# Four edits to a fused three-stage float32 kernel: later out projections in the first mixer, a GpSimd addition, an order on ScalarE, a later key product

## The reference

```python
y = y.reshape(bsz, seq, D_INNER) * jax.nn.silu(z.astype(f32))
y = rmsnorm(y.reshape(bsz, seq, SSD_GROUPS, D_INNER // SSD_GROUPS), gnorm.reshape(SSD_GROUPS, -1))
return y.reshape(bsz, seq, D_INNER).astype(u.dtype) @ w_out
```

## Time and profile before

| | us |
|---|---|
| median of 3 runs (1792.98 to 1796.91) | 1793.48 |
| the profiled execution, its own time | 1795.42 |
| its span | 1793.7 |
| PE busy | 1693.6 (94%) |
| DVE busy | 1125.9 (63%) |
| ACT busy | 841.1 (47%) |
| POOL busy | 368.6 (21%) |
| mean granted clock of PE, share of full speed | 0.978 |

### The profile page before, as it was taken

How to read it: one execution, slowest core, us unless ns; L and a number is a source line. 1 busy time by engine, 2 the same in 40 slices (tenths; PEclk the granted TensorE clock), 3 DMA queues, 4 the chain that set the end, 5 groups by cost and what they waited for, 6 DMA issues and landing times.

```text
span 1793.7 us, 20988 instructions
## 1 busy us (share of the span) xinstructions
PE 1693.6 (94%) x7944; PEld 1361.2 (76%) x7944; DVE 1125.9 (63%) x1520; ACT 841.1 (47%) x1365; POOL 368.6 (21%) x299
## 2 busy tenths in 40 slices
PE   6889999999979999999988899999899999999998
PEld 5667777777757778787866678887688688888886
DVE  6668777788767475756566767777556553434343
ACT  5666565666624354435345335446354442323232
POOL 0254554455541000000006212221220200000001
PEclk9999999999989999999998999999999999999999
DMA  3634444344212222222222323222233333333332
GB/s 105 182 120 127 129 118 140 119 136 123 83 29 82 59 71 71 72 81 70 61 75 60 82 60 82 64 73 88 82 92 98 93 93 96 94 95 102 97 94 71
DMA packets 260106, 164.58 MB, mean 92 GB/s; under 512 B 26909, under 2 KB 249286, under 8 KB 258982
## 3 DMA queue, kind: packets, MB, share of 16 engines
q1 hardware_dynamic: 260006, 163.25, 31.6%
HBM read 160.86 MB, written 2.36 MB: 91 GB/s over the span
## 4 chain that ended last, share of the span: by engine, by line
PE 72%; DVE 14%; ACT 6%; issue 4%; POOL 2%; DMA 1%; SPq 0%; DVEq 0%; ACTq 0%; POOLq 0%
PE stream L79 20%; PE stream L81 20%; PE stream L80 20%; DVE weights_lo L147 2%; DVE ssd_x L987 2%; ACT weights_hi L137 1%; PE q L782 1%; PE q L1969 1%; PE q L1993 1%; PE q L79 1%; PE q L81 1%; PE q L80 1%; DVE ssd_m L1065 1%; PE q L809 1%; POOL h_sum_of_squares L220 1%
## 5 line engine op out<-in xcount | busy, mean ns | idle before, releaser
L79 PE MATMUL stream<-u_lo,weights_hi 128*128 128x512 f32 (+2 forms) x1312 | 533.7, 407 | 12.1 <-DVE u_lo L249 4.5
L81 PE MATMUL stream<-u_hi,weights_hi 128*128 128x512 f32 (+2 forms) x1312 | 516.2, 393 | 0.0
L80 PE MATMUL stream<-u_hi,weights_lo 128*128 128x512 f32 (+2 forms) x1312 | 516.0, 393 | 0.0
L147 DVE TENSOR_TENSOR weights_lo<-weights_raw,weights_hi 128x1024 fp32r<-128x1024 f32 (+4 forms) x269 | 329.4, 1226 | 274.6 <-ACT weights_hi L137 274.2
L137 ACT ACTIVATE weights_hi<-weights_raw 128x1024 fp32r<-128x1024 f32 (+4 forms) x269 | 268.8, 1001 | 462.8 <-PE stream L81 435.3
L79 PEld LDWEIGHTS stream<-u_lo,weights_hi 128*128 128x128 f32 (+2 forms) x1312 | 248.4, 189 | 78.2 <-issue 11.0
L80 PEld LDWEIGHTS stream<-u_hi,weights_lo 128*128 128x128 f32 (+2 forms) x1312 | 248.9, 190 | 54.9 <-issue 4.7
L81 PEld LDWEIGHTS stream<-u_hi,weights_hi 128*128 128x128 f32 (+2 forms) x1312 | 248.0, 189 | 55.6 <-issue 0.7
L217 POOL COPY h_sum_of_squares<-h_squares 128x512 f32<-128x512 f32 x5 | 3.3, 650 | 798.5 <-ACT h_squares L205 798.5
L79 PE MATMUL stream<-mlp_a_lo,weights_hi 128*128 128x512 f32 x256 | 100.2, 391 | 0.0
L81 PE MATMUL stream<-mlp_a_hi,weights_hi 128*128 128x512 f32 x256 | 99.7, 389 | 0.0
(11 more groups left out here) (460 smaller groups left out, 2884.5 us busy)
## 6 DMA issues: line engine op xcount, KB each, us to landing
weights_raw<-in_w_mlp_dram SPq DMA_DIRECT2D x64, 512.0 KB, 3.8
weights_raw<-in_ssd_w_in_dram SPq DMA_DIRECT2D x48, 512.0 KB, 4.1
weights_raw<-in_gla_w_in_dram SPq DMA_DIRECT2D x40, 512.0 KB, 3.8
ssd_cum_steps<-ssd_cum_rows SPq DMA_DIRECT2D x32, 512.0 KB, 5.0
weights_raw<-in_w_in_dram SPq DMA_DIRECT2D x29, 512.0 KB, 3.8
ssd_exp_cum<-ssd_cum_pairs SPq DMA_DIRECT2D x16, 512.0 KB, 7.7
weights_raw<-in_ssd_w_out_dram SPq DMA_DIRECT2D x16, 512.0 KB, 3.6
weights_raw<-in_gla_w_out_dram SPq DMA_DIRECT2D x13, 512.0 KB, 3.4
```

Source lines behind the costliest of these rows:

```text
L79: pe.matmul(out, lh, rl, start=first, stop=False, skip_group_check=skip)
L80: pe.matmul(out, ll, rh, start=False, stop=False, skip_group_check=skip)
L81: return pe.matmul(out, lh, rh, start=False, stop=last, skip_group_check=skip)
L147: dve.tensor_tensor(lo, raw_view(c, n), hi.bitcast(F32), ALU.subtract).then_inc(c.w_split, 1)
```

## The change

The out projections of the first mixer move one round later, except at the end: (g, half) for g up to 4 to (g+3, 4) and (g+3, 7); group 5 to (8, 2) and (8, 5), group 6 to (9, 0) and (9, 2), group 7 stays at (9, 4) and (9, 7). `y_hi` and `y_lo` get two sets, by the parity of the group. The second set takes the place of tensors that only the first rounds use, and since the second mixer's tables lie there later, POOL's set-up of them waits for one more signal. For groups 0 to 6 POOL adds the two tiles of squares, and PE then needs one matmul of ones instead of two. In the second mixer ACT scales both tiles of an out unit ahead of their squares. In the third block the joining product, and the two copies of its result, come one step later.

```diff
-SSD_AT = {(g, half): (g + 2, 4 + 3 * half) for g in range(SG) for half in range(2)}
-SSD_AT[SG - 2, 1] = (SG + 1, 0)
+SSD_AT = {(g, half): (g + 3, 4 + 3 * half) for g in range(SG - 3) for half in range(2)}
+SSD_AT.update({(SG - 3, 0): (SG, 2), (SG - 3, 1): (SG, 5), (SG - 2, 0): (SG + 1, 0), (SG - 2, 1): (SG + 1, 2),
+               (SG - 1, 0): (SG + 1, 4), (SG - 1, 1): (SG + 1, 7)})
...
+        early.close()
         main = ctx.enter_context(ExitStack())
         mb = lambda n, s, d=F32: main.enter_context(nc.sbuf_tensor("ssd_" + n, s, d))
+        y_even = [mb("y_hi_even", [P, 2, T], F32R), mb("y_lo_even", [P, 2, T], F32R)]
...
-        yh, yl = mb("y_hi", [P, 2, T], F32R), mb("y_lo", [P, 2, T], F32R)
+        yhs, yls = [y_even[0], mb("y_hi", [P, 2, T], F32R)], [y_even[1], mb("y_lo", [P, 2, T], F32R)]
...
@@ GpSimd, slot (i, k)
                 if k == 0 and i - 2 in G:
                     complete(i - 2, 1)
+                if k == 1 and 0 <= i - 2 < SG - 1:
+                    pool.wait_ge(s_sq, 3 * (i - 2) + 2)
+                    pool.tensor_tensor(squares[:, 0, :], squares[:, 0, :], squares[:, 1, :], ALU.add)\
+                        .then_inc(s_sq, 1)
...
-            c.second_mixer_set_up(pool, [(s_nrm, SG), (s_y, 4 * SG), (s_st, 7 * SG), (s_m, 4 * SG)])
+            c.second_mixer_set_up(pool, [(s_nrm, SG), (s_y, 4 * SG), (s_st, 7 * SG), (s_m, 4 * SG),
+                                         (c.tile_done, c.tiles_before[plan[SSD_AT[SG - 2, 1]] + 1])])
...
@@ TensorE, slot (i, 1)
-                    pe.wait_ge(s_sq, 2 * f + 2)
-                    for p in range(2):
-                        last = pe.matmul(q[4][:, :], c.ones[:, :], squares[:, p, :], start=p == 0, stop=p == 1)
+                    tiles = 1 if f < SG - 1 else 2
+                    pe.wait_ge(s_sq, 3 * f + (3 if tiles == 1 else 2))
+                    for p in range(tiles):
+                        last = pe.matmul(q[4][:, :], c.ones[:, :], squares[:, p, :], start=p == 0, stop=p == tiles - 1)
...
@@ ScalarE, slot (i, 3)
-                    if f:
-                        act.wait_ge(c.tile_done, c.tiles_before[plan[SSD_AT[f - 1, 1]] + 1])
-                    act.activation(yh[:, :, :], y[:, :, :], ACT.Copy).then_inc(s_yh, 1)
+                    if f >= 2:
+                        act.wait_ge(c.tile_done, c.tiles_before[plan[SSD_AT[f - 2, 1]] + 1])
+                    act.activation(yhs[f % 2][:, :, :], y[:, :, :], ACT.Copy).then_inc(s_yh, 1)
...
@@ second mixer, ScalarE
                     for m in range(m0, m0 + tiles):
+                        scale_tile(c, act, nx, m, free_value(c, out_tile(GH - 1, m)))
+                    for m in range(m0, m0 + tiles):
                         final = free_value(c, out_tile(GH - 1, m))
-                        scale_tile(c, act, nx, m, final)
                         square_tile(c, act, m, final)
                         square_tile(c, act, m, final, gain)
...
@@ third block: TensorE, then ScalarE and VectorE
-                if k == 7:
+                if k == 8:
                     pe.wait_ge(s_tb, 13)
                     pe.wait_ge(s_jn, 4)
                     pe.matmul(q[2][:, :], join[:, :], krt[:, :], start=True, stop=True).then_inc(s_j, 1)
...
-                if k == 8:
+                if k == 9:
                     act.wait_ge(s_j, 1)
...
-                if k == 8:
+                if k == 9:
                     dve.wait_ge(s_kh, 1)
```

More of the change, by code:

```diff
@@ L335, in ssd_stage @@
         cum_pairs = nc.dram_tensor("ssd_cum_pairs", (2, SG, 2, 2, T), F32, kind="Internal").ap()
-        dt, la, cum = sb("dt", [64, T]), sb("la", [64, T]), sb("cum", [64, T])
-        lac, cumc = sb("la_cols", [P, NT, 64]), sb("cum_cols", [P, NT, 64])
+        early = ctx.enter_context(ExitStack())
+        eb = lambda n, s: early.enter_context(nc.sbuf_tensor("ssd_" + n, s, F32))
+        dt, la, cum = eb("dt", [64, T]), eb("la", [64, T]), eb("cum", [64, T])
+        lac, cumc = eb("la_cols", [P, NT, 64]), eb("cum_cols", [P, NT, 64])
         s_v, s_a, s_t = sem("dt_dve"), sem("dt_act"), sem("dt_t")
@@ L789, in _ @@
                     if (i, k) in SSD_OUT:
-                        pe.wait_ge(s_yl, SSD_OUT[i, k][0] + 1)
+                        of = SSD_OUT[i, k][0]
+                        pe.wait_ge(s_yl, of + 1)
+                        yh, yl = yhs[of % 2], yls[of % 2]
                         stream_products(c, pe, n, lambda j: yh[:, j, :], lambda j: yl[:, j, :])
@@ L851, in _ @@
                 pi, pk = before(i, k)
-                if (pi, pk) in plan and pk in CONV:
+                if pi in G and pk in CONV:
                     cj = CONV[pk]
@@ L1023, in _ @@
                     dve.wait_ge(s_yh, f + 1)
-                    dve.tensor_tensor(yl[:, :, :], y[:, :, :], yh[:, :, :].bitcast(F32), ALU.subtract)\
+                    dve.tensor_tensor(yls[f % 2][:, :, :], y[:, :, :], yhs[f % 2][:, :, :].bitcast(F32), ALU.subtract)\
                        .then_inc(s_yl, 1)
```

## The result

The changed kernel takes 1796.19 us (median of 20 runs, 1793.48 to 1800.29) against 1793.18 us (median of 20, 1791.90 to 1796.91). The ratio is 1.0018, 95% interval 1.0011 to 1.0024: 3.2 us slower, just inside the 0.2% that I had set as "no change", where I had forecast 10 us faster. The changed kernel's executions lie in two groups by the granted clock: nine at 0.980 to 0.984 of full take 1793.5 to 1795.9 us, nine at 0.978 take 1798.0 to 1800.3 us, two lie between, and the profiled one, 1800.04 us, is of the upper group.

A forecast was written before the change was run, and what follows sets the result against it. PE, busy in 94% of the span, was taken to bound the kernel. Front -11.1 + 6.2, tail 0 and square sums -5.2 gave -10.1 us, a median of 1783.4 us; range 1777.5 to 1790.

The forecast's parts named there:

- The sums of squares: First mixer, groups 0 to 6: one ones matmul of two goes, 0.86 us each, six counted here, -5.2 us.
- nothing is late there: Middle rounds: `work` comes about 0.8 us later, but `m` of slot 2 follows the norm, which gains 0.86.
- here that falls into DVE's 10 free us of 50: Middle rounds: DVE loses up to an addition's length per round to the shared port, absorbed by its free time.
- The front: Round 2: two units fewer give -11.1 us, and PE's uncovered wait for late decay steps costs +6.2.
- The tail: Rounds 8 and 9: 0 us, with 11.1 us more work covering old waits; bounds -3 and +4.
- The third contribution waits 0.9 for the copy of state: Round 8: PE waits 0.9 us, the copy standing on DVE behind the last three `close` and `y_lo`.
- my bound of +4: Tail's upper bound: two new waits bring another slow stretch of 2.4 us and POOL's items hold DVE's.
- no wait for `m`: Round 8: the unit at (8, 2) covers root, norm and `m`, so PE does not wait there.
- 2.75 for h: Tail: PE's old wait of 2.75 us for a bank of h would still be there.
- 1.9 for `y_lo`: Tail: PE's wait of 5.23 us for `y_lo` of group 7 would fall to about 2.
- Scale and square, join: Second mixer's end and third block's joining product: 0 us each, bounds -1 to +2 and -0.8 to +0.7.
- The slower rival: Slot (i, 1) of seven rounds: PE waits for a late addition on POOL; 1797 us, or 1814; chance 0.03.

The follow-up runs named there:

- the delayed join: Changed kernel with GpSimd's second addition of decay-step halves waiting for VectorE's weight rest in rounds 3 to 7; ratio 0.9994 to the kernel before.
- steps-early kernel: Changed kernel with the decay steps of rounds 1 and 2 asked for one unit earlier on the sync queue; ratio 0.9980 to the kernel before.
- closing first: Changed kernel with the first out tile added to h ahead of the weight rest in slot 4, rounds 3 to 7; ratio 0.9992 to the kernel before.
- the small edits alone: Kernel before with only scaling ahead of squaring in the second mixer and the third block's key product one slot later; ratio 0.9998.

## Why the prediction was wrong

**The sums of squares: predicted -5.2, got a loss.** PE's part was right: one matmul, no wait in front of it, an addition of 1.30 us. The step that failed is "nothing is late there", and with it "here that falls into DVE's 10 free us of 50". Free time in a stretch is an average. VectorE has none between the weight rest and the closing in slot 4, because PE's fourth tile waits for that closing. The rounds went from 57.79 to 58.13 instead of 56.93: 1.2 us each against the forecast, 6.0 in rounds 3 to 7 of the miss of 13. Both single-part kernels show it (58.16 with the addition alone, 57.79 without it), and the delayed join shows that it is the join which holds up the rest. That the order of start decides is what the rows of seven kernels show. With the addition alone the whole is 3.6 us slower where the price was -6.0. I had seen such a stretched operation and the rule of the shared port, and asked only whether the addition itself would be late. I did not ask which pairs of operations on the two engines start within 0.1 us of each other, and what stands behind the one that loses. Those two rows stood in the trace before, 383.78 and 383.84.

**The front: predicted -5.8 for round 2 with its square sum, got -3.7.** Mechanism as described, sizes off, 2.1 us of the miss: the wait was 5.50 and not 4.3, since the steps were issued at 158.05 and not 156.6 (and landed 5.8 us later, as in the trace before), and the contribution waited 1.55 for the state copy and not 0.7. The steps-early kernel confirms that SP's order by units sets this wait, in round 1 too, where it had been all along.

**The tail: predicted 0, got +3.4 to +6.1.** "The third contribution waits 0.9 for the copy of state" failed: it waited 3.90. I put three closings and `y_lo` ahead of the copy at their undisturbed times, and not a product of scores stretched to 1.75 us by GpSimd, nor the norm's two products of 2.62 us ahead of all. Putting the copy first did not help. It only moved the wait, so I take the term that was mis-sized to be the pace of VectorE with GpSimd in that stretch, into which I had put two units' closings; this is argued and no run shows it. By the prediction's own count, from round 8's sums to unit (7, 0), the stretch is 49.4 us (478.62 to 528.02) for 42.5. 1.5 us of the wait are the addition's. The rest of the excess in the profiled execution is the clock, low from 491 to 497.5 us. In executions where the clock recovers early the stretch takes 82.35 us (closing first, same order here). The fair partner isn't the 80.39 us of the kernel before, whose clock was 0.85, but the small edits alone, with the order of the kernel before in this stretch:
```profile
472.58:551.54 78.96, 60.18 (x267) 0.91 0.20 53
```
That is +3.4, within my bound of +4. Steps that held: no wait for `m`, 2.75 for h, 1.9 for `y_lo`.

**Scale and square, join: predicted 0 each, measured together 0.4 us faster, +-1.6.** Right, for the two together.

**Together** the three parts miss by 6.0 + 2.1 + 3.4 to 6.1, that is 11.5 to 14.2 us, for a miss of 13.3 (3.2 for -10.1). The moved units by themselves, front and tail, were to bring -4.9 and brought -0.5 +-1.6.

**The slower rival** has 1797 us, next to the 1796.2 measured, by luck. It named the addition, but at the wrong place: PE never waited for it. The loss came through a pair of operations 21 us further on, which no rival of mine held.

What stays open: how long the clock stays low behind equal waits. The same stretch with the same order took 82.35, 82.40, 82.85, 86.27 and 86.52 us in the profiled executions of five kernels. Nor did I show by which steps 1.3 us on GpSimd in slot 1 become 0.1 us in slot 5. In the changed kernel the join no longer waits for ACT (its cut ended at 380.27, the join started at 380.45, right behind L744), where before it waited until 383.84 for a cut that ended at 383.76; counted from the end of that cut, the join starts 0.17 us behind it instead of 0.08, and the weight rest 0.21 instead of 0.02, so both come later and the rest by more. This is what the rows show, and no run separates it.

## What to carry to other kernels

Before work is moved to GpSimd, list in the trace the pairs of VectorE and GpSimd operations on two SBUF inputs that start within the shift which the move makes, and follow what stands behind each VectorE one; a free share of 20% says nothing about the one place where PE waits. If such a pair decides, put the operation that PE waits for ahead of it on VectorE, or hold GpSimd's back: 4.7 and 4.3 us here, each by a few lines. And where loads are tied to units of work, look at what a slot without a unit does to the load behind it: asking one unit earlier was worth 6.8 us on the changed kernel, more than either part of the change was to bring (5.2 and 4.9). It was not tried on the kernel before, whose round 1 has the same wait.

## What the runs showed of the hardware

A swing of 0.1 us in the start of a weight rest against a join moves 1.0 to 1.1 us from one engine to the other, and in a loop it does so in every round the same: rounds 4 to 7 agree within 0.1 us in every kernel here (58.12 to 58.15 in the changed one), while the whole kernel spreads over 7 us between executions. Kernels that are alike in these rounds agree too: their mean is 57.78 to 57.79 us in the three in which the rest goes first, and 58.13 to 58.16 in the four in which the join does. So a mechanism in a loop can be read from one profile to 0.05 us per round, and the tail, where the clock falls behind waits, cannot (82.35 to 86.52 us above). The operation that loses is stretched by nearly the winner's remaining time: 2.33 for 1.22 beside a join with 1.25 left, 2.30 for 1.29 beside a rest with 1.16 left.
